# In each attention slot the waiting unit's values come ahead of the first transposes in TensorE's program

## The chip, the cores and the metric

The kernel runs on one core of a Trainium2 chip. The metric is the device time of one execution in microseconds (us). Three timed runs of the kernel before gave 1783.25, 1787.11 and 1788.55 us, median 1787.11. The engines are called as in the profile: PE is TensorE's matmul side and PEld its weight loads, DVE is VectorE, ACT is ScalarE, POOL is GpSimd and SP is SyncE.

## The reference, cut to what matters

One decoder layer over 1024 tokens of width 1024: a modulated norm, an input projection, three token mixers side by side, their gated sum, an output projection, then a routed mixture of experts. The change is in the mixers. For each block of 128 query tokens they compute, in the words of the reference:

```python
s = jnp.einsum('bqghd,bkgd->bghqk', qb, kw) * scale        # scores, per head
p = masked_softmax(s - alibi * dist, mask)                 # 8 window heads, 8 selected-block heads
o_win = jnp.einsum('bghqk,bkgd->bqghd', p, vw)             # values, per head
# sliding-window heads (4, with sinks): the same with keys of two blocks
# stick-breaking heads (4): a = exp(z + reversed sums of -softplus(z)), then a @ v
# compressed keys: one score matrix for all 8 heads, whose sum picks 8 key blocks
```

## The kernel before, in words

The attention stage lies at about 345 to 1092 us of the span. There are eight query tiles n = 0 to 7 of 128 tokens. Each tile is written out as 20 slots, i = 0 to 19, and slot number q = 20n + i. A slot has one unit (kind and head): eight `win` units (window heads, at most five key blocks of 128), eight `slc` units (selected blocks, n + 1 key blocks) and, at i = 6, 9, 12 and 15, one `swa` unit (at most two key blocks). These four slots also carry a ride, a stick-breaking (`sb`) unit with n + 1 key blocks. Slot i = 0 has the compressed scores `cmp` too.

A unit passes through four steps. PE computes its scores into PSUM, with a mask added by a last small bf16 matmul (line 1973; `swa` has none). DVE takes the row maximum (L1469), ACT the exponential (L1030), which signals `p_ok`. PE transposes the probabilities, one 128x128 f32 matmul per key block (L2000), into PSUM banks 4 and 5 in groups of four blocks that alternate between the banks. ACT copies the even groups (L422) and DVE the odd ones (L424) into SBUF; this is called the evacuation below. PE multiplies them with the values (L2032), two matmul records per key block of 64 columns each, and signals `pv_done`.

The steps of three units overlap. In slot q, PE's program has in this order: the scores of unit q; the transposes T of unit q - 1; the values V of the unit that was transposed last before it and is "waiting"; a third of a gate matmul group G (eight f32r matmuls of 512 columns, L2049 to L2066), which is ordinary projection work spread over slots; the scores of the ride. In i = 10, 13, 16, 19 the ride of four slots earlier is transposed as well, behind G, and in i = 3, 4, 5 the compressed probabilities, the finished output of the previous tile and the block selection. Where such a second transposition is there, the values of the first unit follow it. 144 slots carry G; none do in slot 0 of tiles 4 to 7, in q = 74 and 75, and from q = 152 on.

ACT and DVE have programs of their own, also by slots. ACT in slot q: exponential of unit q, then the evacuation of what slot q transposes (so the copy of unit q - 1 stands behind the exponential of unit q), then work of the rides, then the copies for the gate groups (L1068 empties G's bank, L1004 rounds the next gate weights, L999 rounds half of the tokens once at q = 73). DVE in slot q: maximum of unit q, evacuation, gathering of finished outputs, the scan of a ride two slots after it (L1518, L1520), gate weights. PE's waits stand on the first weight load of a step: T waits for `p_ok`, V for the evacuation of all its groups, and at a few places for a gathered output.

Of the kernel before, what the change touches and what calls it, by code (L numbers as in the profile page):

```python
# [68 lines left out]
def hybrid_trunk(nc, x, c, w_ada, b_ada, g_norm_mix, g_norm_moe, w_in, cmp_pe_k, cmp_w1_k, cmp_w2_k, cmp_pe_v,  # L69
                 cmp_w1_v, cmp_w2_v, nsa_q_gain, nsa_k_gain, swa_q_gain, swa_k_gain, swa_sinks, w_branch_a,  # L70
                 w_branch_b, w_branch_c, w_out, w_router, router_bias, w_exp_gate, w_exp_up, w_exp_down, out):
    _, T, D = x.shape
    NT, NK = T // P, D // P
    NE, DE = w_exp_gate.shape[1], w_exp_gate.shape[3]
# [18 lines left out]
    with ctx:  # L93
# [1687 lines left out]
        def _(pe):  # L1781
# [194 lines left out]
            def transposes(u):  # L1976
                k, n = u["kind"], u["n"]
                if k == "cmp":
                    pe.wait_ge(cmp_pok, n + 1)
                    src = cmp_p  # L1980
                elif k == "sel":
                    pe.wait_ge(sel_ok, n + 1)
                elif k == "out":
                    pe.wait_ge(o_read, 5 * n + 5)
                    src = o_tok
                elif k == "sb":
                    pe.wait_ge(pb_ok, n * SB_H + u["h"] + 1)
                    src = prob_b
                else:
                    pe.wait_ge(p_ok, u["slot"] + 1)  # L1990
                    src = prob[u["slot"] % 2]
                for j, g in enumerate(u["groups"]):
                    bank, blocks = group(u, j)
                    if g >= 2:
                        wait_evacuated(pe, g - 2)
                    for c, t in enumerate(blocks):
                        if k == "sel":
                            ins = pe.transpose(bank[0:AUG, 0:P], sel[:, :], ident[:, :])
                        else:
                            ins = pe.transpose(bank[:, c * P:(c + 1) * P], src[:, t * P:(t + 1) * P], ident[:, :])  # L2000
                    ins.then_inc(t_full, 1)

            def values(u):
                k, n, h = u["kind"], u["n"], u["h"]
                for g in u["groups"]:
                    wait_evacuated(pe, g)
                pt = probT[u["v"] % 2]

                if k == "cmp" and n:
                    pe.wait_ge(o_read, 5 * n)  # L2010
                elif k == "win" and n and h == 0:
                    pe.wait_ge(o_read, 5 * n - 2)
                elif k == "slc" and h == 0:
                    pe.wait_ge(o_read, 5 * n + 2)
                elif k in ("sb", "swa") and h == 0:
                    pe.wait_ge(o_read, 5 * n + 1)
                if k == "cmp":
                    for g in range(NSA_H // 2):
                        mm = pe.matmul(psum[:, 6, g * P:(g + 1) * P], pt[:, g * P:(g + 1) * P], v_cmp[:, :],
                                       start=True, stop=True)  # L2020
                    mm.then_inc(pv_done, 1)
                    return
                bank, c = {"win": (7, h), "slc": (7, h), "swa": (6, h), "sb": (6, SWA_H + h)}[k]
                for j in range(u["nb"]):
                    t = u["lo"] + j
                    if k in ("win", "slc"):
                        v = (v_win if k == "win" else v_slc)[:, t, :]
                    elif k == "swa":
                        v = v_c[:, t, (h // 2) * HD:(h // 2 + 1) * HD]
                    else:  # L2030
                        v = v_b[:, t, h * HD:(h + 1) * HD]
                    mm = pe.matmul(psum[:, bank, c * HD:(c + 1) * HD], pt[:, j * P:(j + 1) * P], v,  # L2032
                                   start=(j == 0), stop=(j == u["nb"] - 1))
                mm.then_inc(pv_done, 1)

            def gate_matmuls(q):

                g, c = gate_steps(q)
                if c is None:
                    return  # L2040
                hf = gate_of(g)[0]
                hi, lo = hT_hi[hf], hT_lo[hf]
                if c == 0:
                    pe.wait_ge(h_lo_ok, 2 * hf + 1)
                    pe.wait_ge(gw_hi_ok, 2 * g + 1)
                    if g:
                        pe.wait_ge(z_ok, g)
                    for k in range(4):
                        pe.matmul(GATE_BANK, gate_hi[0][:, k, :], hi[:, k, :], start=(k == 0), stop=False)  # L2049
                        mm = pe.matmul(GATE_BANK, gate_hi[0][:, k, :], lo[:, k, :], start=False, stop=False)  # L2050
                    mm.then_inc(gate_first, 1)
                elif c == 1:
                    pe.wait_ge(gw_lo_ok, 2 * g + 1)
                    for k in range(4):
                        pe.matmul(GATE_BANK, gate_piece(2 * g, 1)[:, k, :], hi[:, k, :], start=False, stop=False)
                    pe.wait_ge(gw_hi_ok, 2 * g + 2)
                    pe.wait_ge(h_hi_ok, 2 * hf + 2)
                    for k in range(4):
                        pe.matmul(GATE_BANK, gate_hi[1][:, k, :], hi[:, 4 + k, :], start=False, stop=False)
                else:  # L2060
                    pe.wait_ge(h_lo_ok, 2 * hf + 2)
                    for k in range(4):
                        pe.matmul(GATE_BANK, gate_hi[1][:, k, :], lo[:, 4 + k, :], start=False, stop=False)  # L2063
                    pe.wait_ge(gw_lo_ok, 2 * g + 2)
                    for k in range(4):
                        mm = pe.matmul(GATE_BANK, gate_piece(2 * g + 1, 1)[:, k, :], hi[:, 4 + k, :], start=False, stop=(k == 3))  # L2066
                    mm.then_inc(g_full, 1)

            waiting = None
            for q, s in enumerate(slots):  # L2070
                for u in s["S"]:
                    if u is not s["ride"]:
                        scores(u)
                for j, u in enumerate(s["T"]):
                    if j == 1:
                        gate_matmuls(q)
                    if waiting and "v" not in u:
                        values(waiting)
                        waiting = None
                    transposes(u)  # L2080
                    if waiting:
                        values(waiting)
                    waiting = u if "v" in u else None
                if s["ride"]:
                    scores(s["ride"])
                if len(s["T"]) < 2:
                    gate_matmuls(q)
# [190 lines left out]
```

## Time and profile before

| | us |
|---|---|
| median of 3 runs | 1787.11 |
| the profiled execution, its own time | 1787.33 |
| its span | 1785.5 |
| PE busy | 1672.9 (94%) |
| PEld busy | 1302.6 (73%) |
| DVE busy | 1024.2 (57%) |
| ACT busy | 732.8 (41%) |
| mean granted clock of PE | 0.97 |

The span is the stretch from the first to the last instruction of the program; 1.8 us of the execution lie around it. Busy time of PE counts matmuls by modelled ends, so it can be near 100% where matmuls are short and separated by weight loads. The start times of instructions are measured: the distance between two starts is what the argument uses.

### The profile page before, as it was taken

How to read it: one execution, taken by the hardware profiler on the slowest of the kernel's cores; microseconds unless marked ns; L12 is line 12 of the kernel's file. 1: busy time of each engine (PE TensorE's matmuls, PEld its weight loads, DVE VectorE, ACT ScalarE, POOL GpSimd, SP SyncE). 2: the span in 40 equal slices, each digit the busy share in tenths (PEclk: the TensorE clock that was granted, in tenths of full speed). 3: DMA queues.
4: the chain of work that ended last, by engine and by line, in shares of the span. 5: the costliest groups of instructions: out<-in, count | busy, mean ns of one | idle time of the engine just before them, and what ended most of it. 6: DMA issues, size and time to landing. Idle time of an engine off the chain costs nothing.

```text
span 1785.5 us, 23790 instructions
## 1 busy us (share of the span) xinstructions
PE 1672.9 (94%) x8573; PEld 1302.6 (73%) x8573; DVE 1024.2 (57%) x1665; ACT 732.8 (41%) x1272; POOL 364.4 (20%) x342
## 2 busy tenths in 40 slices
PE   6999999699999999999999988999939999999996
PEld 5555464477778778888878877888828888888885
DVE  5564442535465555566565565775485565656485
ACT  1421110344545545545455553331133544545473
POOL 2211133000000001101020110000022434346355
PEclk9999999699999989999999989999959999999998
DMA  9415360032222111121111113752266887878794
GB/s 339 151 47 188 118 165 24 13 95 71 71 72 72 53 37 54 54 54 54 36 54 36 42 54 118 282 189 106 99 244 188 271 268 260 270 258 298 239 376 125
DMA packets 146955, 247.68 MB, mean 139 GB/s; under 512 B 6424, under 2 KB 69984, under 8 KB 145536
## 3 DMA queue, kind: packets, MB, share of 16 engines
q1 hardware_dynamic: 138544, 217.81, 35.8%
q0 software_dynamic: 8112, 27.93, 6.5%
q8 instruction: 65, 1.06, 0.3%
q10 hardware_dynamic: 192, 0.54, 0.1%
q14 instruction: 42, 0.34, 0.1%
HBM read 210.60 MB, written 36.18 MB: 138 GB/s over the span
## 4 chain that ended last, share of the span: by engine, by line
PE 80%; DVE 9%; DMA 4%; issue 3%; ACT 3%; POOL 1%; SPq 0%; ACTq 0%; DVEq 0%; POOLq 0%
PE psum L1866 10%; PE psum L2032 7%; PE psum L1970 5%; PE psum L2211 5%; PE psum L2212 5%; PE psum L2216 5%; PE psum L2000 5%; PE psum L1886 3%; PE psum L2254 2%; PE psum L2255 2%; PE psum L2259 2%; DMA arena<-in_w_in_dram 2%; PE psum L2049 2%; PE psum L2063 2%; PE psum L2066 2%
## 5 line engine op out<-in xcount | busy, mean ns | idle before, releaser
L805 POOL TENSOR_SCALAR arena<-arena 128x128 f32<-128x128 f32 (+7 forms) x32 | 71.1, 2222 | 667.9 <-ACT arena L1057 352.3
L2032 PE MATMUL psum<-kv,arena 128*128 128x64 f32 x1464 | 192.1, 275 | 2.2 <-ACT arena L422 2.2
L2032 PEld LDWEIGHTS psum<-kv,arena 128*128 128x128 f32 x1464 | 187.0, 198 | 4.9 <-ACT arena L422 2.9
L1866 PE MATMUL psum<-arena 128*128 128x512 f32 (+2 forms) x512 | 189.0, 522 | 0.3 <-DVE arena L1219 0.3
L1469 DVE TENSOR_REDUCE negm<-psum 128x1 f32<-128x640 f32 (+7 forms) x128 | 90.2, 705 | 113.1 <-PE psum L1973 112.7
L2211 PE MATMUL psum<-heads_r,kv_r 128*128 128x512 f32 x384 | 150.9, 393 | 3.4 <-DVE kv_r L1736 3.4
L1866 PEld LDWEIGHTS psum<-arena 128*128 128x128 f32 x512 | 95.9, 192 | 77.4 <-issue 73.8
L1730 DVE TENSOR_TENSOR arena_r<-arena,heads_r 128x2048 fp32r<-128x2048 f32 x64 | 142.5, 2287 | 15.1 <-ACT heads_r L1130 15.1
L2212 PE MATMUL psum<-heads_r,kv_r 128*128 128x512 f32 x384 | 150.6, 392 | 0.0
L2000 PE MATMUL psum<-ident,arena 128*128 128x128 f32 x828 | 133.5, 284 | 17.4 <-ACT arena L1030 12.3
L1030 ACT ACTIVATE arena<-psum,negm 128x640 f32<-128x640 f32 (+7 forms) x128 | 89.3, 697 | 135.8 <-DVE negm L1469 135.2
L851 POOL TENSOR_TENSOR arena_r<-arena,bc_r 128x2048 fp32r<-128x2048 f32 x16 | 103.3, 6455 | 104.8 <-ACT bc_r L1130 104.8
L2000 PEld LDWEIGHTS psum<-ident,arena 128*128 128x128 f32 x828 | 94.8, 146 | 35.8 <-ACT arena L1030 15.2
L1130 ACT ACTIVATE heads_r<-arena 128x2048 fp32r<-128x2048 f32 x64 | 117.3, 1913 | 7.4 <-DMA out_dram<-heads 4.2
L424 DVE COPY arena<-psum 128x512 f32<-128x512 f32 (+3 forms) x140 | 69.0, 493 | 50.4 <-PE psum L2000 50.4
L2216 PE MATMUL psum<-arena_r,kv_r 128*128 128x512 f32 x384 | 95.0, 389 | 0.0
L1004 ACT ACTIVATE arena_r<-arena 128x512 fp32r<-128x512 f32 x96 | 60.0, 626 | 81.4 <-DMA arena<-in_w_in_dram 73.9
L422 ACT ACTIVATE arena<-psum 128x512 f32<-128x512 f32 (+3 forms) x140 | 65.5, 468 | 52.6 <-PE psum L2000 52.6
L2211 PEld LDWEIGHTS psum<-heads_r,kv_r 128*128 128x128 f32 x384 | 72.9, 190 | 19.0 <-issue 3.7
L2212 PEld LDWEIGHTS psum<-heads_r,kv_r 128*128 128x128 f32 x384 | 72.9, 190 | 15.2
L2216 PEld LDWEIGHTS psum<-arena_r,kv_r 128*128 128x128 f32 x384 | 72.1, 188 | 15.0
L1970 PE MATMUL psum<-arena_r,heads_r 128*128 128x256 f32 (+2 forms) x192 | 72.4, 379 | 8.5 <-ACT arena L1057 4.4
(441 smaller groups left out, 3468.0 us busy)
## 6 DMA issues: line engine op xcount, KB each, us to landing
arena<-in_w_exp_gate_dram SPq DMA_DIRECT2D x16, 2048.0 KB, 12.0
arena<-in_w_exp_down_dram SPq DMA_DIRECT2D x16, 2048.0 KB, 12.5
arena<-in_w_exp_up_dram SPq DMA_DIRECT2D x16, 2048.0 KB, 13.9
arena<-in_w_in_dram SPq DMA_DIRECT2D x48, 512.0 KB, 4.2
arena<-in_w_ada_dram SPq DMA_DIRECT2D x7, 2048.0 KB, 11.1
z_dram<-arena SPq DMA_DIRECT2D x48, 256.0 KB, 2.3
arena<-z_dram SPq DMA_DIRECT2D x8, 1536.0 KB, 7.5
bc<-in_w_ada_dram SPq DMA_DIRECT2D x4, 2048.0 KB, 8.4
```

The costliest lines, as they stand in the source:

```text
L851: pool.tensor_tensor(ew_lo(e, 2)[:, SLOT // 2:SLOT], w_raw(e, 2)[:, SLOT // 2:SLOT], ew_hi[2][:, SLOT // 2:SLOT].bitcast(F32), ALU.subtrac ...
L1030: act.activation(prob[q % 2][:, 0:w], src, ACT.Exp, bias=negm[:, q % 4:q % 4 + 1], accum_out=den[:, u["n"] % 2, col:col + 1]).then_inc(p_o ...
L1130: act.activation(ew_hi[i][:, cs], w_raw(e, i)[:, cs], ACT.Copy).then_inc(w_hi_ok, 1)
L1469: dve.tensor_reduce(m1, score_buf(u)[:, 0:w], AX.X, ALU.max, negate=True).then_inc(max_ok, 1)
L1730: dve.tensor_tensor(ew_lo(e, i)[:, cs], w_raw(e, i)[:, cs], ew_hi[i][:, cs].bitcast(F32), ALU.subtract).then_inc(w_lo_ok, 1)
L1866: mm = pe.matmul(psum[:, 4 + s % 3, 0:w], hT[:, k, n * P:(n + 1) * P], slot(slot_of(L_TOK + ch))[:, k, 0:w], start=(k == 0), stop=(k == NK ...
L1970: mm = pe.matmul(b[:, c0:c1], lhs, keys[:, k0 + c0:k0 + c1], start=(i == 0), stop=not masks and i == len(pairs) - 1)
L2000: ins = pe.transpose(bank[:, c * P:(c + 1) * P], src[:, t * P:(t + 1) * P], ident[:, :])
L2032: mm = pe.matmul(psum[:, bank, c * HD:(c + 1) * HD], pt[:, j * P:(j + 1) * P], v, start=(j == 0), stop=(j == u["nb"] - 1))
L2211: pe.matmul(out, xs_hi[:, k, :], w_hi[:, k, :], start=(k == 0), stop=False)
L2212: pe.matmul(out, xs_lo[:, k, :], w_hi[:, k, :], start=False, stop=False)
L2216: mm = pe.matmul(out, xs_hi[:, k, :], w_lo[:, k, :], start=False, stop=(k == NK - 1))
```

## The change

Where a slot has a unit waiting for its values and something to transpose, the values used to be issued behind the first transposition (except ahead of a transposition without values, `sel` or `out`). Now they are issued ahead of the slot's first transposition. Transposes, values, their waits and signals are the same instructions; no other engine's program changes.

```diff
                 for j, u in enumerate(s["T"]):
                     if j == 1:
                         gate_matmuls(q)
-                    if waiting and "v" not in u:
+                    if waiting and (j == 0 or "v" not in u):
                         values(waiting)
                         waiting = None
                     transposes(u)
```

## Rows read from the trace of the kernel before

**Rows 1.** The page's first part: busy us (share) and instructions of each engine.
```profile
PE 1672.9 (94%) x8573; PEld 1302.6 (73%) x8573; DVE 1024.2 (57%) x1665; ACT 732.8 (41%) x1272; POOL 364.4 (20%) x342
```
**Rows 2.** Stretch, us; PE, PEld, DVE, ACT, POOL busy; clock; DMA; GB/s.
```profile
857.00:966.00 109.00, 108.20 (x702) 89.52 (x701) 63.85 (x106) 55.25 (x107) 13.24 (x4) 1.00 0.19 51
...
345.00:1092.00 747.00, 715.13 (x4380) 586.66 (x4380) 419.82 (x812) 367.36 (x808) 72.09 (x39) 0.97 0.20 54
```
**Rows 3.** PE's waits in 345 to 1092 us: total us, times, longest.
```profile
PE psum L2000 <- ACT arena L1030: 12.3, 11, 3.9
PE psum L1970 <- ACT arena L1057: 4.4, 3, 3.0
```
**Rows 4.** PE in order of time, slot q = 91: start, us, line, count.
```profile
710.36 0.23 PE L1973 MATMUL psum<-tri_causal,identb 128*128 128x128 bf16 x1
710.43 0.72 PE L2000 MATMUL psum<-ident,arena 128*128 128x128 f32 x5
710.98 1.23 PE L2032 MATMUL psum<-kv,arena 128*128 128x64 f32 x10
712.02 0.71 PE L2063 MATMUL psum<-arena_r 128*128 128x512 f32 x2
```
**Rows 5.** PEld in the same slot.
```profile
710.38 0.53 PEld L2000 LDWEIGHTS psum<-ident,arena 128*128 128x128 f32 x5
710.88 1.20 PEld L2032 LDWEIGHTS psum<-kv,arena 128*128 128x128 f32 x10
```
**Rows 6.** PE in order of time, 680.75 to 684.6 us (end of q = 84, start of 85).
```profile
680.75 0.72 PE L2032 MATMUL psum<-kv,arena 128*128 128x64 f32 x5
681.31 1.04 PE L2000 MATMUL psum<-ident,arena 128*128 128x128 f32 x8
682.11 0.36 PE L1970 MATMUL psum<-arena_r,heads_r 128*128 128x256 f32 x1
...
682.99 0.71 PE L2000 MATMUL psum<-ident,arena 128*128 128x128 f32 x5
683.46 1.17 PE L2063 MATMUL psum<-arena_r 128*128 128x512 f32 x4
```
**Rows 7.** All engines in order of time, slot q = 28.
```profile
443.11 0.37 ACT L422 ACTIVATE arena<-psum 128x256 f32<-128x256 f32 x1
...
443.26 0.44 PE L2000 MATMUL psum<-ident,arena 128*128 128x128 f32 x2 [1.41 <-ACT arena L1030]
...
443.53 0.66 PE L2032 MATMUL psum<-kv,arena 128*128 128x64 f32 x4
```
**Rows 8.** PE in order of time, slot q = 75.
```profile
629.25 0.70 PE L1970 MATMUL psum<-bc 64*128 64x256 f32 x2
632.39 1.12 PE L2000 MATMUL psum<-ident,arena 128*128 128x128 f32 x4 [2.45 <-ACT arena L1030]
633.30 1.81 PE L2032 MATMUL psum<-kv,arena 128*128 128x64 f32 x8
```
**Rows 9.** The same view and columns as Rows 2, behind slot q = 75.
```profile
632.00:636.00 4.00, 3.61 (x13) 3.03 (x14) 0.00 (x0) 2.64 (x8) 0.00 (x0) 0.55 0.30 90
636.00:640.00 4.00, 4.00 (x15) 2.44 (x14) 1.96 (x4) 1.38 (x3) 0.00 (x0) 0.50 0.00 0
640.00:644.00 4.00, 4.00 (x19) 3.33 (x18) 2.29 (x2) 0.09 (x1) 0.00 (x0) 0.67 0.01 2
```
**Rows 10.** DVE in order of time, slot q = 117.
```profile
842.55 0.42 DVE L424 COPY arena<-psum 128x256 f32<-128x256 f32 x1
```
**Rows 11.** ACT in order of time, slot q = 118.
```profile
849.86 0.58 ACT L422 ACTIVATE arena<-psum 128x512 f32<-128x512 f32 x1
```
**Rows 12.** PE in order of time, slot q = 119.
```profile
850.84 0.23 PE L1973 MATMUL psum<-tri_causal,identb 128*128 128x128 bf16 x1
```
**Rows 13.** All engines in order of time, slot q = 155.
```profile
1047.03 0.58 ACT L422 ACTIVATE arena<-psum 128x512 f32<-128x512 f32 x1
...
1047.18 1.14 PE L2000 MATMUL psum<-ident,arena 128*128 128x128 f32 x8 [0.70 <-ACT arena L1030]
```

## The prediction

> **What bounds the kernel now.** First the page's busy times [rows 1]: PE is at 94% of the span and no other engine above 57%, so time is won where PE waits or where its instructions follow each other badly. Second the stretches of the attention stage, the only stage that the change touches [rows 2]: in 345 to 1092 us PE is busy for 715.1 of 747 us; in tile 6 (857 to 966) it is 108.2 of 109 at a granted clock of 1.00. So only 31.9 us of idle time are there to be filled. Third PE's waits [rows 3]: the largest, 12.3 us in 11 times, is T waiting for an exponential. The longest of these, 3.9 us, is in slot 1, where no unit is waiting yet; so at most 8.4 us are within reach. The next, scores waiting for ACT (4.4 us), is not touched. Fourth, since PE is full, the start times inside one slot: what counts is the distance between instructions, not busy time.
>
> **Part 1, the order itself.** The edit removes nothing and adds nothing on any engine; it issues no DMA and moves past no queue of SP or POOL. In 144 slots (all from q = 2 to 160 but i = 6 of each tile and i = 5 of tiles 1 to 7) V and T change places. Old order, slot 91 [rows 4]: the last mask matmul starts at 710.36, T 0.07 later at 710.43, V at 710.98, G at 712.02, in all 1.66 us. The modelled length of a T record is 0.27 and of a V record 0.275, so the starts of T's five span 0.72 - 0.27 = 0.45, and those of V's ten 1.23 - 0.275 = 0.955. From the last T start (710.88) to V are 0.10 to 0.11; from the last V start (711.935) to G are 0.085. The loads explain this [rows 5]: V's first load starts at 710.88, with the last T, and is hidden beside it. V's ten loads stand (1.20 - 0.19) / 9 = 0.112 apart. At that pace the ten matmuls would span 1.008; they span 0.955, so one of the nine distances, the first, is 0.055 short.
>
> New order, by transitions that occur elsewhere [rows 6]. V to T: five V from 680.75 have their last start at 680.75 + 0.72 - 0.275 = 681.195, T follows at 681.31, 0.115 later. T to scores: eight T have their last start at 681.31 + 1.04 - 0.27 = 682.08, the scores follow at 682.11, 0.03 later. T to G: last T start 682.99 + 0.71 - 0.27 = 683.43, G at 683.46, again 0.03. A G behind T is as slow from its first to its second start as one behind V: (1.17 - 0.39 - 2 x 0.23) = 0.32 and 0.71 - 0.39 = 0.32. So a step behind T costs 0.03 where a step behind V costs 0.085, since its load is hidden beside the longer T. The sum of the joints: old 0.07 + 0.105 + 0.085 = 0.26; new x + 0.115 + 0.03, with x from mask to V. x is nowhere in the trace. Its load can start no earlier than T's, so I take x = 0.07, as for T; the sum is 0.215, a gain of 0.045 to 0.05. That V's first distance stays short is the second unknown: if it does not, the slot loses 0.055 again and the gain is nothing. With x = 0.03 (as T to G) and the distance short, the gain is 0.09. I take 0.05, because the load of T's second block follows its first just as fast behind the mask as elsewhere.
>
> How many slots collect it: 144, less 12 in which T waits for an exponential, less about 12 more of tile 0, where the wait of the next slot eats it, 120. 120 x 0.05 = **6.0 us gained**; ends 0 and 120 x 0.09 = 10.8.
>
> The Trainium skill, "TensorE: Matmul & The Clock Gate", section "Measured speedup vs the span model", says that a weight load overlaps with matmuls in flight only when it goes to another row group. All loads here use the full 128 rows; by that rule no order hides a load and the sum would be 1787.3 - 0.8, given as a rival below. The trace speaks against it: the load of 710.88 lies beside a T whose successor starts on time, 0.10 later [rows 4, 5].
>
> **Part 2, values in the wait for the exponential.** Where T waits and V's evacuation is done, V now runs in the wait. The largest is q = 75 [rows 8]: scores start at 629.25, T at 632.39, with 2.45 us idle. V's unit (four blocks, eight records, 0.9 us at the full clock) was transposed in q = 74. That slot has no G, so T's move behind V makes its evacuation late by at most 0.9 us, to about 0.5 us into the idle time; V still fits whole. Gain 0.9. Four more slots (q = 7, 23, 43, 55) have this pattern with V of 0.2 to 0.65 us: together 1.5. **2.4 us gained**, if what makes the exponential late is not itself waiting for PE. In tiles 0 to 3 it mostly is ACT waiting for a gate weight DMA, which T's place does not move. Ends: 0 (the exponential moves too) and 3.2 (every one of the 8.4 us with a V of mean length in it).
>
> **Part 3, the wait that V brings.** In ACT's program the evacuation of the waiting unit stands behind the exponential for which T waits. Where the exponential is late, V in front waits longer than T did, and T, the scores and everything in PE's queue stand behind it. In q = 28 [rows 7] the evacuation ends at 443.11 + 0.37 = 443.48 and V starts at 443.53, T at 443.26. In the new order V starts at 443.53 too, and T comes behind it: its two starts (0.23) less 0.05, loss 0.18. q = 22 is alike. Six slots of tile 0 have one block, loss 0.06 each, 0.35. In q = 155 [rows 13] T starts at 1047.18; V could at 1047.03 + 0.58 + 0.05 = 1047.66, loss 0.48 - 0.05 = 0.43. Slot q = 81 has an evacuation ending 0.34 behind its mask matmul: 0.3. Sum **1.4 us lost**.
>
> **Part 4, a later evacuation.** T now ends later by V's length (0.224 us per key block, up to 1.8 us in tile 7). Ordinary slots do not feel it: ACT's evacuation is held by the exponential ahead of it. DVE feels it where it copied at once. In q = 117 the copy starts at 842.55 [rows 10], at once behind DVE's maximum and only 0.24 behind its transposes; it would be late by 1.34 - 0.24 = 1.1, a scan stands behind it, and DVE has 0.45 us of idle time before the next maximum (both distances by pairing this slot's records). So the exponential of q = 118 is 0.65 late. In q = 119 the evacuation ends at 849.86 + 0.58 = 850.44 [rows 11] and the mask starts at 850.84 [rows 12]: 0.4 of slack, loss 0.25. The slots i = 3 and those behind a ride's transposes (i = 11, 14, 17) have 0.1 to 0.6 of slack in tiles 4 to 7 but the delay before them is 0.3 or nothing. For places like q = 17 of the other tiles slack is above the delay. **0.3 us lost**; ends 0 and, were each of 20 such slots late by 0.6, 12.
>
> **Sum.** The profiled execution took 1787.3 (span 1785.5 and 1.8 around it), 0.2 above the median, which lies in the middle of it all. 1787.3 - 6.0 - 2.4 + 1.4 + 0.3 = **1780.6**.
>
> **The rivals.**
> - *Nothing in the joints.* V's first distance behind the mask is 0.112, or no load is hidden there. Only parts 2 to 4 are left: 1787.3 - 0.7 = 1786.6. For it: mask to V is nowhere in the trace, and 0.055 decides. Against: every V in a slot has the short first distance, behind T as behind G. 0.22.
> - *The clock.* Behind the wait of q = 75 the granted clock is at its lower level, 1.2 GHz: 0.55, 0.50 and 0.67 in the next three stretches of 4 us [rows 9], that is 4 x (0.45 + 0.50 + 0.33) / 0.50 = 10.2 us at half speed, 5.1 us of work lost. PE had been idle for 2.45 us before. With V in the wait this idle time is 0.9 shorter and in two pieces; PE waited 1.41 in q = 28 [rows 7]. If the fall goes, 1780.6 - 5 = 1775.6. Against: the total of idle time there stays above 1.4. 0.2.
> - *Slower: the evacuation becomes the bound.* V in front turns ACT's order (exponential, then copy) and DVE's scans into PE's wait, in tiles 4 to 7 where part 4 gives slack of 0.1 to 0.6. It decides once the copy comes later by more than that slack. At 0.6 lost in each of 20 slots: 1780.6 + 12 = 1792.6, before any fall of the clock that such waits bring. For it: DVE is near full in scan slots, tile 7 has no G to cover from q = 152. Against: in tile 7 both copies already come 1.9 us and more behind their transposes in most slots from q = 153 on (paired in the same way). 0.15.
> - *The order in PE's queue is not what the edit says*, since evacuations or semaphores of another unit hold V anyway: within 0.3% of before. 0.03.
>
> **How the numbers follow.** My forecast has 0.4. A measurement can tell 0.3%, 5.4 us, from no change, so faster means under 1781.7. The forecast lies at this line: 0.26 of its 0.4 fall below. With the clock's 0.19: faster 0.45. The rest of the forecast, nearly all of the first rival and part of the others: same 0.4; slower 0.15. Range 1774 to 1791: it takes in the clock case, the gain of 10.8 in part 1, nothing in the joints, and the slow case up to two thirds of its price. The likeliest case's own range is 1778 to 1784.
>
> **What would show it.** In a slot like q = 91: mask, V 0.07 later, T 0.115 behind V's last start, G 0.03 behind T's last; the whole 0.05 shorter than 1.66; in V the first distance short. PE's waits: T behind the exponential down from 12.3 to about 8, V behind ACT's copy up from 2.2 by about 2. In q = 75 V ahead of the idle time or in it, and the clock behind it. I am wrong if the new waits of V are above 4 us in tiles 4 to 7, or if full tiles such as tile 6 keep their 109 us; tile 6 should lose 18 x 0.05 = 0.9.

## The result and the profile after

The changed kernel takes 1796.24 us (median of 4 runs, 1794.28 to 1797.45); four runs of the kernel before, the three above and one more, have a median of 1785.18 (1781.75 to 1788.55). The ratio is 1.0057, interval 1.0042 to 1.0073: some 10 us slower, outside the forecast range on the slow side. The profiled execution took 1794.28, its span is 1792.5. Ratios, here and below, leave out two executions that stand far off, 2816.2 us of the kernel before and 2190.68 of the last experiment (mean granted clock 0.73).

Nothing was added to any engine. First part of the page after, against [rows 1]:

```profile
PE 1675.7 (93%) x8573; PEld 1301.7 (73%) x8573; DVE 1028.6 (57%) x1665; ACT 734.3 (41%) x1272; POOL 366.1 (20%) x342
```

**The order is what the edit says, and its joints gain nothing.** PE after in order of time, slot q = 91, against [rows 4]: V (L2032) ahead of T (L2000), then G. The clock is at its full level in both traces.

```profile
705.54 0.23 PE L1973 MATMUL psum<-tri_causal,identb 128*128 128x128 bf16 x1
705.61 1.28 PE L2032 MATMUL psum<-kv,arena 128*128 128x64 f32 x10
706.72 0.72 PE L2000 MATMUL psum<-ident,arena 128*128 128x128 f32 x5
707.20 0.47 PE L2063 MATMUL psum<-arena_r 128*128 128x512 f32 x1
```

From the mask to G are 707.20 - 705.54 = 1.66, exactly what it was. Mask to V is 0.07. V's last start is 705.61 + 1.28 - 0.275 = 706.615 and T follows 0.105 later; T's last start is 706.72 + 0.45 = 707.17 and G follows 0.03 later. All this is as forecast. But V is 0.05 longer, 1.28 for 1.23: its nine distances are now (1.28 - 0.275) / 9 = 0.112 each, the first too. Over the slots at the full clock and without a wait (about 100) the medians are 0.068 + 0.112 = 0.180 from the mask to V's second start. Over the 88 of them that have G behind and can be paired, the whole from mask to G is 0.437 after and 0.435 before, V's and T's further distances left out.

**PE's waits moved on to the scores.** PE's waits after in 345 to 1095 us (total, times, longest), against [rows 3]:

```profile
PE psum L1970 <- ACT arena L1057: 9.5, 6, 4.1
PE psum L2000 <- ACT arena L1030: 7.0, 3, 3.9
PE psum L2032 <- ACT arena L422: 5.3, 9, 1.2
PE psum L1970 <- ACT arena L1030: 5.0, 5, 2.4
PE psum L2032 <- DVE arena L424: 1.2, 3, 0.9
```

T (L2000) waits 5.3 us less for the exponential. V (L2032) waits 6.5, which was 2.2 for ACT's copy before: 4.3 more. The net of the two is -1.0 us, as that of parts 2 and 3; each is larger than said there. New is the first line: the scores (L1970) wait 9.5 for ACT's copy L1057, which was 4.4, and 1.6 more for the exponential.

**Where the time goes by slot.** I took for each slot the end of its scores in both traces and looked at where the difference steps. 1.4 of the 7.0 us by which this profile is longer are there before slot 0 ends and are none of the change's. Up to q = 75 the profile gains 1.2, and 5.7 more at q = 76 and 77, where the low clock of [rows 9] is gone. Then come losses at i = 13 of each later tile: 0.56 at q = 93, 1.12 at 113, 1.17 at 133, 2.14 at 153; and 0.93 at q = 154, 1.20 at 156. Steps of 0.1 to 0.4 stand at i = 2 to 4. The last values of the stage start at 1091.28 and wait there; the attention ends at 1093.2, before at 1086.1, and 3.8 of these 7.1 us arise behind the scores of q = 159.

Steps of one pair of profiles need a check against the others. In the profiles of the kernels below that have the old order in tiles 0 to 3, the difference to the kernel before up to q = 75 is -0.6 to -3.1, and with the new order -0.5 to -4.4: the 1.2 is scatter. The steps at q = 93, 113 and 133 are in every profile with the new order in i = 11 and DVE's program as it was, and in no other. The 0.93 at q = 154 and about 0.5 of the 2.14 at 153 come in profiles with the old order there too (0.8 and 0.6 in the last experiment), so they are not the change's.

**The chain behind a step,** q = 111 to 113. DVE after, from the maximum of q = 111 to that of the `swa` unit of q = 112:

```profile
805.15 0.96 DVE L1469 TENSOR_REDUCE negm<-psum 128x1 f32<-128x768 f32 x1 [0.81 <-PE psum L1973]
...
807.15 0.42 DVE L424 COPY arena<-psum 128x256 f32<-128x256 f32 x1 [1.04 <-PE psum L2000]
...
809.38 1.76 DVE L1518 TENSOR_TENSOR_SCAN arena<-arena 128x768 f32<-128x768 f32 x1
811.17 0.96 DVE L1520 TENSOR_TENSOR arena<-arena 128x768 f32<-128x768 f32 x1
...
813.11 0.21 DVE L1467 TENSOR_SCALAR negm<-negm,sink 128x1 f32<-128x1 f32 x1
```

The same before:

```profile
809.07 0.96 DVE L1469 TENSOR_REDUCE negm<-psum 128x1 f32<-128x768 f32 x1 [0.80 <-PE psum L1973]
809.94 0.41 DVE L424 COPY arena<-psum 128x256 f32<-128x256 f32 x1
...
815.89 0.21 DVE L1467 TENSOR_SCALAR negm<-negm,sink 128x1 f32<-128x1 f32 x1
```

Counted from the reduction, DVE's copy comes 2.00 behind it after and 0.87 before: it waits 1.04 for transposes that now stand behind V. Gather, scan and product follow without a gap, so the maximum of q = 112 comes 7.96 behind the reduction, before 6.82: 1.14 late, undiminished. ACT after:

```profile
813.36 0.29 ACT L1028 ACTIVATE sink_e<-sink,negm 128x1 f32<-128x1 f32 x1 [1.88 <-DVE negm L1467]
...
814.05 0.57 ACT L422 ACTIVATE arena<-psum 128x512 f32<-128x512 f32 x1
814.53 0.83 ACT L1051 ACTIVATE arena<-arena 128x768 f32<-128x768 f32 x1
815.45 0.81 ACT L1057 ACTIVATE arena<-psum 128x768 f32<-128x768 f32 x1
```

The exponential waits 1.88 (0.68 before, as the row of ACT shows):

```profile
816.14 0.29 ACT L1028 ACTIVATE sink_e<-sink,negm 128x1 f32<-128x1 f32 x1 [0.68 <-DVE negm L1467]
```

Behind it in ACT's program stands the copy L1057, which takes the ride's scores out of the PSUM banks that the next scores need (in tiles 4 to 7 the program puts both in banks 0 and 1, so the chain can stand there alone). PE after, end of q = 112 and start of 113:

```profile
813.16 0.23 PE L1973 MATMUL psum<-tri_strict,identb 128*128 128x128 bf16 x1
813.19 1.17 PE L2055 MATMUL psum<-arena_r 128*128 128x512 f32 x4
814.20 1.08 PE L2059 MATMUL psum<-arena_r 128*128 128x512 f32 x4
816.32 0.50 PE L1970 MATMUL psum<-arena_r,heads_r 128*128 128x512 f32 x1 [1.04 <-ACT arena L1057]
```

PE has finished G and stands idle for 1.04 until L1057 is done. Before, the same scores start without a wait:

```profile
817.06 1.17 PE L2055 MATMUL psum<-arena_r 128*128 128x512 f32 x4
...
819.10 0.50 PE L1970 MATMUL psum<-arena_r,heads_r 128*128 128x512 f32 x1
```

These rows also correct a sentence ahead of the prediction. I had written that G stands ahead of the ride's scores. In slots with one transposition it stands behind them: S, T, V, ride's scores, G, next scores. So G is what covers L1057, and where there is no G, from q = 152 on, nothing does.

### The profile page after: what moved, and what is told of

It reads as the page before. It is cut to its first block and busy times, and to the rows that moved or that the text cites. A ratio compares the mean times of both kernels' runs of the same rounds, so it can differ in the third digit from the quotient of the medians.

```text
span 1792.5 us, 23790 instructions
## 1 busy us (share of the span) xinstructions
PE 1675.7 (93%) x8573; PEld 1301.7 (73%) x8573; DVE 1028.6 (57%) x1665; ACT 734.3 (41%) x1272; POOL 366.1 (20%) x342
## 5 line engine op out<-in xcount | busy, mean ns | idle before, releaser
L2032 PE MATMUL psum<-kv,arena 128*128 128x64 f32 x1464 | 199.5, 280 | 6.5 <-ACT arena L422 5.3
L2032 PEld LDWEIGHTS psum<-kv,arena 128*128 128x128 f32 x1464 | 186.6, 198 | 17.8 <-ACT arena L422 7.6
L2000 PE MATMUL psum<-ident,arena 128*128 128x128 f32 x828 | 132.0, 283 | 11.5 <-ACT arena L1030 7.0
L2000 PEld LDWEIGHTS psum<-ident,arena 128*128 128x128 f32 x828 | 103.2, 155 | 21.9 <-ACT arena L1030 7.5
L1970 PE MATMUL psum<-arena_r,heads_r 128*128 128x256 f32 (+2 forms) x192 | 73.5, 385 | 15.2 <-ACT arena L1057 9.5
```

The lines of the kernel that those rows point to most:

```text
L1970: mm = pe.matmul(b[:, c0:c1], lhs, keys[:, k0 + c0:k0 + c1], start=(i == 0), stop=not masks and i == len(pairs) - 1)
```

## The experiments

Each kernel is the changed one with the condition of the edit cut down to some slots, or with the place of one gather moved; each computes the whole layer. The diffs are against the changed kernel. Each was timed beside the kernel before on the same chip: the first four beside 17 runs of it (median 1785.68), the next four beside 35 (1785.43), the last three beside 29 (1787.07). Ratios are to the kernel before, with 95% intervals. Steps by slot are those of the one profiled execution, against the profile of the kernel before.

**Old order in i = 11 alone.**

```diff
-                    if waiting and (j == 0 or "v" not in u):
+                    if waiting and ((j == 0 and q not in (91, 111, 131, 151)) or "v" not in u):
```

> Values first in all slots but i = 11 of tiles 4 to 7, which keep the old order. Theory A (the copy of the later transposes delays DVE's gather and scan in slot 11, so the maximum and exponential of slot 12, the ride's copy on ACT and the PSUM bank for the scores of slot 13): the waits of about 0.6 to 2.1 us before the scores of i = 13 go back to those of before, 4 to 6 us of the 11 come back, about 1791. Theory B (the loss is the tail without gate groups, q >= 152, and its clock): 0 to 1 us, about 1795.5. Theory C (small losses in each of the 144 slots, joints and V's own wait): less than 0.5 us.

Measured: 1791.79 (1791.05 to 1796.44, 6 runs), ratio 1.0044 [1.0029, 1.0058]. The steps at q = 93, 113 and 133 are gone and that at 153 is down to 0.61; 1.00 at 154 and 1.20 at 156 stay. The chain is confirmed, but taking it away gives back 2.3 us by the ratios, less than the 4 to 6 that were expected of it.

**New order in i = 11 alone.**

```diff
-                    if waiting and (j == 0 or "v" not in u):
+                    if waiting and ((j == 0 and q in (91, 111, 131, 151)) or "v" not in u):
```

> The old order everywhere but in slot i = 11 of tiles 4 to 7 (four slots). Theory A: these four slots alone cost 4 to 6 us, about 1790. Theories B and C: within 0.5 us of the kernel before, 1785 to 1786.

Measured: 1792.25 (1786.27 to 1796.83, 6 runs), 1.0045 [1.0030, 1.0060]. Four slots of 144 make the kernel 8 us slower (5.4 to 10.7 by the interval). The steps are 0.56 (93), 1.16 (113), 1.17 (133), 1.96 (153), in all 4.85. There are others where the program is that of before: -1.83 at q = 76, -2.09 at 154 and 0.76 at 156. A step of -2.3 at 154 is also in two later kernels with the old order there, and one of 0.8 in two others: this slot scatters by 3 us from profile to profile. The rows of the chain are there, DVE's late copy and then PE's wait (one line of each engine):

```profile
807.53 0.42 DVE L424 COPY arena<-psum 128x256 f32<-128x256 f32 x1 [1.04 <-PE psum L2000]
```

```profile
816.69 0.50 PE L1970 MATMUL psum<-arena_r,heads_r 128*128 128x512 f32 x1 [1.10 <-ACT arena L1057]
```

The profiled execution was the fastest of the six, with 1786.27; the others are up to 10.6 above it. What varies between them, the trace of one can't show.

**Old order from q = 152 on,** where no G covers.

```diff
-                    if waiting and (j == 0 or "v" not in u):
+                    if waiting and ((j == 0 and q < 152) or "v" not in u):
```

> Values first only below q = 152; the last eight slots, which have no gate group, keep the old order. Theory B: most of the 11 us comes back, 1787 or less. Theory A: only what lies behind slot 152, the longer waits of i = 16 and the last V's wait for its copy (about 1 us) with the clock they bring, 3 to 5 us, about 1792. Theory C: 0.5 us.

Measured: 1794.29 (1791.23 to 1797.19, 6 runs), 1.0051 [1.0035, 1.0067]. The steps at i = 13 are all there (0.56, 1.14, 1.17, 2.14); those at 154 and 156 are gone, and one of 0.93 stands at 159. The end alone doesn't make the loss: 1.1 us come back, where 3 to 5 were expected of it.

**The gather one slot earlier.** In i = 11 DVE gathers the window heads' output between its copy and the scan. Done in i = 10, it leaves room for a copy that is 1.1 late. PE's program stays as changed.

```diff
-                if i == 11 and n < NT:
+                if i == 10 and n < NT:
                     gather_output(n, "win")
```

> The changed kernel with DVE's gathering of the window output moved from slot 11 to slot 10 of each tile. Theory A: DVE has 1.75 us less to do ahead of the maximum of slot 12, so the waits before the scores of i = 13 vanish in tiles 4 to 6 and shrink to under 1 us in tile 7: 5 us or more back, 1791 or less. Theories B and C: no difference, 1796.

Measured: 1790.94 (1788.45 to 1794.32, 11 runs), 1.0032 [1.0023, 1.0042], some 4.5 us below the changed kernel by the ratios. DVE of this kernel:

```profile
805.90 0.41 DVE L424 COPY arena<-psum 128x256 f32<-128x256 f32 x1
806.23 1.75 DVE L1518 TENSOR_TENSOR_SCAN arena<-arena 128x768 f32<-128x768 f32 x1
```

The scan stands 0.33 behind the copy instead of 2.23. PE of this kernel:

```profile
811.84 1.17 PE L2055 MATMUL psum<-arena_r 128*128 128x512 f32 x4
812.85 1.08 PE L2059 MATMUL psum<-arena_r 128*128 128x512 f32 x4
813.76 0.39 PE L1970 MATMUL psum<-arena_r,heads_r 128*128 128x512 f32 x1
```

The scores of q = 113 don't wait. The steps of tiles 4 to 6 at i = 13 are gone; 0.53, 0.98 and 1.20 at q = 153, 154 and 156 stay, of which only the last is the order's. So the route is through DVE's program: the same V ahead of T makes the scores of i = 13 wait no longer in tiles 4 to 6 once DVE has room.

**The same with the old order at the end.**

```diff
-                if i == 11 and n < NT:
+                if i == 10 and n < NT:
...
-                    if waiting and (j == 0 or "v" not in u):
+                    if waiting and ((j == 0 and q < 152) or "v" not in u):
```

> Values first below q = 152 only, and the gathering of the window output in slot 10. Theory A holds two places responsible: slot 11 of tiles 4 to 7, and in tile 7 the slots without a gate group. Both are taken away here, so the time is that of the kernel before, 1784 to 1787. Were there a loss in each of the other slots (theory C, 0.03 us or more each), or a cost of the clock apart from the waits, it stays at 1789 or more.

Measured: 1786.5 (1781.72 to 1792.39, 12 runs), 1.0003 [0.9989, 1.0016]. With both causes out the new order in all other slots costs nothing that can be measured, and it gains nothing either. Two later results say that this is a sum of two small parts of opposite sign (-2.7 in tiles 0 to 3, 2.3 in tiles 4 to 7).

**The gather alone, on the kernel before.**

```diff
-                if i == 11 and n < NT:
+                if i == 10 and n < NT:
...
-                    if waiting and (j == 0 or "v" not in u):
+                    if waiting and "v" not in u:
```

> The kernel before with only the gathering moved to slot 10. The scores of i = 13 wait 1.24 us in tile 7 of the kernel before and nearly not in tiles 4 to 6. Theory A: up to 1.2 us and a part of the clock's fall behind it, 1783 to 1785.5; in the old order DVE now waits in slot 10 for the values behind the transposes, which may cost it 1 us of spare time, no more. A rival says the move in itself gains 5 us, as it seemed to do beside the changed kernel: 1781.

Measured: 1782.1 (1780.06 to 1790.51, 12 runs), 0.9986 [0.9970, 1.0002]. Not told apart from no change, and by its interval (0 to 5.4 us gained) not from the rival's 5 us either. So of the 4.5 us that the gather takes from the changed kernel a part may be its own, 2.5 by the middle of this interval. What shows the route is the trace, where the waits at i = 13 go, and not this time.

**New order from q = 152 on alone.**

```diff
-                    if waiting and (j == 0 or "v" not in u):
+                    if waiting and ((j == 0 and q >= 152) or "v" not in u):
```

> The old order below q = 152, values first in the last slots, which have no gate group. Theory A: the scores of i = 16 wait 1.1 us longer, those of i = 18 about 1.6 longer, the last values 0.9, and the clock falls for longer: 4 to 6 us over the kernel before, 1790 to 1792. Theory C: within 0.5 us of before.

Measured: 1790.99 (1787.67 to 1793.49, 12 runs), 1.0032 [1.0022, 1.0043], 5.7 us. Steps of 0.31 at q = 154, 1.84 at 156, 0.84 at 157, 1.51 at 159, and -0.73 at 158; from the last scores to the end of the stage it takes 4.1 us more than before (3.8 in the three other kernels with V first in the last slots, 0 to 2.8 in those without). PE's waits in 1010 to 1100 us of this kernel: two waits of scores for the exponential, and V for ACT's copy.

```profile
PE psum L1970 <- ACT arena L1030: 3.8, 2, 3.0
...
PE psum L2032 <- ACT arena L422: 1.0, 1, 1.0
```

**New order below q = 80 alone.**

```diff
-                    if waiting and (j == 0 or "v" not in u):
+                    if waiting and ((j == 0 and q < 80) or "v" not in u):
```

> Values first in tiles 0 to 3 alone (q below 80). Theory A expects no wait of its own there: the joints are equal (0.112 for V's first distance behind the mask), the waits for the exponential are 2 us shorter. 1783 to 1786. The forecast's joints (0.05 in each of some 70 slots) would give 1782. Theory C, small losses everywhere: 1787 or more.

Measured: 1783.28 (1779.75 to 1786.95, 12 runs), 0.9985 [0.9972, 0.9998]: 2.7 us gained, interval 0.4 to 5. It is the amount of part 2, and the wait of q = 75 is shorter as it said (1.1 for 2.45 us). But the mean granted clock of these 12 runs is 0.970, and 0.968 in the runs of before beside them: by itself that is worth 2 to 3.5 us (worked out below), so the gain is mostly one of the clock. With at most four blocks V makes no copy late enough to show as a step.

**Both of the gains together.**

```diff
-                if i == 11 and n < NT:
+                if i == 10 and n < NT:
...
-                    if waiting and (j == 0 or "v" not in u):
+                    if waiting and ((j == 0 and q < 80) or "v" not in u):
```

> Values first in tiles 0 to 3 alone, and the window output gathered in slot 10. The two gains measured singly (2.7 and 2.5 us) lie in different tiles; if they add, 1780 to 1781, ratio 0.997. If both are one drift of the measurement, 1783 to 1785.

Measured: 1783.58 (1779.29 to 1787.68, 12 runs), 0.9983 [0.9972, 0.9993]. It beats both kernels, by 3 us before and 13 us after, but not the order alone: the gather's own gain, if there is one, doesn't add.

**One slot, q = 154.**

```diff
-                    if waiting and (j == 0 or "v" not in u):
+                    if waiting and ((j == 0 and q == 154) or "v" not in u):
```

> Values first in one slot alone, i = 14 of tile 7 (q = 154), which has no gate group and whose DVE part holds a scan. Theory A: the eight blocks of values ahead of the transposes make DVE's copy and scan about 1.1 us later, so the scores of i = 16 (q = 156) wait 1.1 us longer, and the fall of the clock behind them is longer: 1 to 3 us over the kernel before. If the tail's loss comes from ACT's copies of outputs or from the last slots instead: nothing at q = 156.

Measured: 1788.05 (1786.54 to 1790.73, 12 runs), 1.0010 [1.0000, 1.0019]. One V ahead of one T makes a step of 1.20 at q = 156, and 1.00, -1.00 and 0.56 behind it, in all 1.8 us in the trace and 1.8 in the ratio (0 to 3.4 by the interval). PE's waits in 1010 to 1100 us, before and in this kernel:

```profile
PE psum L1970 <- ACT arena L1057: 4.2, 2, 3.0
```

```profile
PE psum L1970 <- ACT arena L1057: 5.1, 2, 3.8
```

The longest wait for L1057 grows by 0.8. It is the chain of i = 11 once more, as DVE of this kernel shows in q = 154 and 155:

```profile
1041.93 0.69 DVE L424 COPY arena<-psum 128x512 f32<-128x512 f32 x1 [1.01 <-PE psum L2000]
1042.54 2.28 DVE L1518 TENSOR_TENSOR_SCAN arena<-arena 128x1024 f32<-128x1024 f32 x1
...
1048.73 0.21 DVE L1467 TENSOR_SCALAR negm<-negm,sink 128x1 f32<-128x1 f32 x1
```

The copy waits for transposes behind V, the scan of a ride stands behind the copy, the maximum of the `swa` unit of q = 155 behind that, then the ride's copy L1057 on ACT and the scores of q = 156. Before, the copy of q = 154 waited for nothing:

```profile
1044.42 0.68 DVE L424 COPY arena<-psum 128x512 f32<-128x512 f32 x1
```

**Tiles 4 to 7 up to q = 150, without i = 11.**

```diff
-                    if waiting and (j == 0 or "v" not in u):
+                    if waiting and ((j == 0 and 80 <= q < 151 and q % 20 != 11) or "v" not in u):
```

> Values first in tiles 4 to 7 below q = 151 but for slot 11: some 60 slots. Theory A: nothing waits there but DVE's small delays behind slots 1 and 2 (0.1 to 0.2 each tile): within 1 us of the kernel before. The forecast's joints: 3 us faster. Theory C: 2 us or more slower.

Measured: 1788.97 (1784.24 to 1793.85, 11 runs), 1.0013 [1.0000, 1.0026], 2.3 us slower and on the edge of what the interval tells from nothing. The steps are 0.12 to 0.35 at i = 2 to 4 of tiles 4 to 7, in all 1.5 us up to q = 151. They are small but real: every profile with V first in these slots has them (1.3 to 1.6 in all, the steps at i = 13 left out), and none of the others. Behind q = 151 the order is that of before, and yet this profile has steps of 0.61 at q = 153, 0.80 at 154 and 0.93 at 159.

The four pieces are -2.7, +8.0, +5.7 and +2.3, in all 13.3, where the whole is 10.2. Each has an interval of about 2.5 us to either side, so they agree as a sum. They don't agree when taken away one by one: i = 11 costs 8.0 alone and gives back 2.3, the end costs 5.7 alone and gives back 1.1, both together (with the gather) give back 9.6. My reading is that they share a cost that falls due once, a lower clock in tile 7. The listed runs bear it out in part. Their mean granted clock is 0.968 for the kernel before, and 0.966 with i = 11 alone, with the end alone, and with the whole change: the same fall each time, not twice for both. (It is 0.9665 in the last experiment, where hardly a wait changes, so the waits are not all of it.) What it costs is an estimate: the runs of one kernel get 1.1 us longer for each 0.001 of clock that they lack, which makes 2 us, and (1 - clock) x time makes 3.5. So a fifth to a third of the 10.2 us is the clock's, and the larger part is waits. That the fall lies in tile 7 is not shown.

## Why the prediction was wrong

**Part 1 failed in its second unknown, and rival 1 stated it.** Mask to V was taken as 0.07 and is 0.068; V to T 0.115 (0.112), T to G 0.03 (0.028; medians over the slots). "That V's first distance stays short" is the term that fell: it is 0.112, and with 0.055 a slot the whole 6.0 is gone. The short distance was not a saving that could be carried along. Behind T, V's first start is late (0.109) and its second follows at 0.058, in all 0.167 behind T's last start; behind the mask it is 0.068 + 0.112 = 0.180. The forecast took the early first start of the one and the short distance of the other. The evidence for it was that every V of a unit in the slots had the short distance; but each stood behind a T or a G, so it was the same case each time. The values of the compressed scores (L2019) had 0.112 behind a T in tiles 1 to 7 of the same trace. The choice between 0 and 10.8 was no better than a guess.

The rule of the Trainium skill ("TensorE: Matmul & The Clock Gate", Part 3, section "The mechanism", which stands ahead of the section that the prediction names) is that a weight load overlaps with matmuls in flight only in another row group. By it no order hides a load here, and it gave the result of rival 1, 0.7 us (the 0.8 beside it in the prediction is a slip). The rows still speak against the rule itself: G follows 0.03 behind T and 0.085 behind V, and both loads use all rows.

**Parts 2 and 3 held in their sum, in part by luck.** T's waits fell from 12.3 to 7.0 (forecast 8) [rows 3]. V's waits rose by 4.3, where I had said 2, but part of these replaces T's: the net of both is -1.0, as was the net of 2.4 and 1.4. Of my two signs of being wrong one stayed away, V's new waits in tiles 4 to 7 are 1.4 and not above 4; the other came, tile 6 lost nothing and took 1.6 us more. The new order below q = 80 alone gains 2.7, mostly through the clock. In slot q = 75 V ran in the idle time, against [rows 8]:

```profile
630.36 1.10 PE L2032 MATMUL psum<-kv,arena 128*128 128x64 f32 x8 [0.16 <-DVE arena L424]
...
632.59 0.66 PE L2000 MATMUL psum<-ident,arena 128*128 128x128 f32 x4 [1.12 <-ACT arena L1030]
```

**Part 4 is the step that made the sign wrong.** It says that the copy of DVE comes 1.1 late in a slot like q = 117, and "0.3 us lost". Measured are 4.85 us of steps and 8.0 in time for i = 11 alone, and 5.7 for the end alone. The delay itself is right: 1.13 in q = 111. Two things were wrong. I looked at one place, q = 117, and carried it to the others by their slack; for those behind a ride's transposes, i = 11 among them, I said that the delay was 0.3 or nothing. And as the consumer of the late exponential I took only the evacuation behind it, needed in the next slot behind the scores. Slot q = 118 carries no ride, but q = 112 does: behind its exponential in ACT's program stands L1057, and for that the scores of q = 113 wait, with only G between. A row of the waits pointed to it: the second of [rows 3], scores for L1057, which I set aside as "not touched". It was the one to ask what feeds it.

**The slow rival named the engine, not the place.** "The evacuation becomes the bound" was given 1792.6, and it decided by slack as it said, but by 20 slots at 0.6. Measured are four slots at 0.56 to 1.96 where i = 11 has the new order alone, and the end. Its argument against, that in tile 7 both copies come 1.9 behind their transposes anyway, counts slots from q = 153 on one by one; the chain in them starts where a scan stands behind the copy. The other place of the loss was named in a sentence of the same rival: "tile 7 has no G to cover from q = 152".

**The clock.** The fall behind q = 75 went in this profile. PE after in 632 to 636 and 636 to 640, against [rows 9]; the last number but two is the granted clock:

```profile
632.00:636.00 4.00, 3.41 (x21) 2.22 (x21) 0.90 (x5) 3.44 (x9) 0.00 (x0) 1.00 0.35 104
636.00:640.00 4.00, 4.00 (x28) 3.33 (x26) 4.00 (x6) 2.25 (x5) 1.38 (x1) 1.00 0.01 2
```

But it came and goes with the execution. The kernel with the old order in i = 11 has the same program as the changed one up to q = 90, and its profile has the fall again; the same two stretches of it:

```profile
632.00:636.00 4.00, 4.00 (x17) 2.72 (x16) 1.02 (x2) 2.81 (x7) 0.00 (x0) 0.62 0.04 12
636.00:640.00 4.00, 4.00 (x14) 3.12 (x13) 3.23 (x3) 0.27 (x2) 0.00 (x0) 0.53 0.01 2
```

So a fall in one profile shouldn't be priced as one of the kernel; all profiles together say more. At q = 76 to 80 the seven with the new order in q = 75 gain 1.0, 2.5 (four times) and 5.7 (twice) against the profile of before; of the five others with the old order four gain 0 to 0.2 and one 1.6. So the change does gain there, some 2.5 us, of which 1.2 are the shorter idle time and the rest is the clock. The rival of the clock was right about the place, and about its whole price in two profiles of seven.

In the tail one pair of profiles misleads in the same way. From 1030 to 1095 us the granted clock is 0.83 before and 0.79 after, but 0.74 in the last experiment and 0.71 with both gains together, which have the old order there. What the order does to the clock can be read only from the mean of many runs, as above. The waits are steadier. PE in the tail, before:

```profile
1034.43 0.50 PE L1970 MATMUL psum<-arena_r,heads_r 128*128 128x512 f32 x1 [1.24 <-ACT arena L1057]
...
1055.12 0.50 PE L1970 MATMUL psum<-arena_r,heads_r 128*128 128x512 f32 x1 [2.99 <-ACT arena L1057]
```

after:

```profile
1034.87 0.80 PE L1970 MATMUL psum<-arena_r,heads_r 128*128 128x512 f32 x1 [2.73 <-ACT arena L1057]
...
1057.92 0.80 PE L1970 MATMUL psum<-arena_r,heads_r 128*128 128x512 f32 x1 [4.08 <-ACT arena L1057]
...
1077.79 0.50 PE L1970 MATMUL psum<-arena_r,heads_r 128*128 128x512 f32 x1 [2.39 <-ACT arena L1030]
...
1091.28 1.97 PE L2032 MATMUL psum<-kv,arena 128*128 128x64 f32 x16 [0.87 <-DVE arena L424]
```

The first of these waits is 2.7 to 2.8 in the three profiles with the new order in i = 11 and the gather in its place, and 1.1 to 1.25 in all others. The second is 3.8 to 4.2 in four of the five with the new order in q = 154, and 3.0 to 3.5 in those without it. The last, of V, is 0.9 in all four with the new order in the last slots and absent elsewhere. The wait of 2.39 is not the order's: it is 2.4 in five profiles with the old order there, and 0.79 in that of before.

**Open** is how much of the tail's loss is the wait and how much the clock behind it, beyond the estimate above. The two come together, and one kernel's runs differ by 3 to 11 us among themselves. An experiment would have to keep PE busy in these waits with work that nobody needs; it wasn't tried.

## What to carry to other kernels

When an instruction moves back on a full engine, follow its consumer's whole program, not only its result: here a copy on DVE that was 1.1 us late cost nothing to the matmuls that read it, and 1.0 to a matmul that waited for PSUM banks, which ACT frees three instructions behind an exponential that the late copy had held up. List the waits that exist, and ask of each what stands ahead of its releaser; an existing short or covered wait is where a delay comes out. A short distance seen in one context only (behind T or G) says nothing of another, however many times it is there; and an order should be chosen by slot, since the same edit gains at a long wait with few blocks moved past (q = 75) and loses where many are. And steps between two profiles are worth little until profiles with and without the change in that slot have been laid side by side.

## What was unexpected of the hardware

A run of f32 values matmuls of 64 columns starts every 0.112 us, whatever stands before it, but for the first distance. That is 0.058 behind f32 transposes, 0.055 behind G, 0.112 behind a bf16 mask matmul and 0.160 behind the last scores of a `swa` unit (medians over 164, 15, 100 and 22 slots at the full clock). How long the record before it lasts doesn't decide it: 0.27, 0.39, 0.23 and 0.38. Where the first distance is short, the first start was late: to the second start it is 0.167 behind a T and 0.180 behind a mask. Why, no run here shows.

A wait of PE doesn't bring a low clock by its length alone. Before, the clock fell behind the wait of 1.24 us at 1034.43; after, it stayed at 1.00 behind one of 1.24 in q = 133, and in q = 75 behind 1.12, which in another profile with the same program up to there was followed by 0.62 and 0.53.
